# Seven-product weight slabs in two more MLPs of a three-block network, and a regrouping in the last MLP

## What is computed

```
first block, two layers:   x = x + mixer(x); x = x + relu(rms_norm(x, g) @ w_in)**2 @ w_out     # 4096 hidden
second block:              x = x + 0.5 * swiglu(rms_norm(x, g), w_gate, w_up, w_down)           # 2816 hidden, ffn1
                           x = x + mixer(x);  then the same swiglu again                        # ffn2
third block:               mod = silu(c) @ w_ada + b_ada       # 1024 x 6144, depends on c alone
                           x = layer_norm(alpha * x + (1 + g) * mixer(x))
                           x = layer_norm(alpha * x + (1 + g) * swiglu(h, w_ffn_in, w_ffn_out)) # ffn3
```

## Time and profile before

| | before |
|---|---|
| median of three runs | 3399.15 us |
| the profiled execution, device time | 3401.31 us |
| its span | 3399.5 us |
| PE busy | 3313.1 us (97%) |
| POOL busy | 1888.2 us (56%) |
| DVE busy | 1792.6 us (53%) |
| ACT busy | 880.2 us (26%) |
| granted TensorE clock, mean | 0.996 |
| DMA | 340.89 MB, mean 100 GB/s |

### The profile page before, as it was taken

How to read it: one execution, slowest core, us unless ns; L and a number is a source line. 1 busy time by engine, 2 the same in 40 slices (tenths; PEclk the granted TensorE clock), 3 DMA queues, 4 the chain that set the end, 5 groups by cost and what they waited for, 6 DMA issues and landing times.

```text
span 3399.5 us, 48354 instructions
## 1 busy us (share of the span) xinstructions
PE 3313.1 (97%) x20166; PEld 2664.7 (78%) x20166; DVE 1792.6 (53%) x2828; ACT 880.2 (26%) x1845; POOL 1888.2 (56%) x1499
## 2 busy tenths in 40 slices
PE   8999999999999999999999998999999999999997
PEld 6767788986778888888788777778887776778996
DVE  6544334548544344333442666564346657568775
ACT  2242011347411112000202532110002125235443
POOL 7526666731256666767675002777665645846652
PEclk9999999999999999999999999999999999999998
DMA  5203334230033432433323002432324635412321
GB/s 175 83 25 112 111 125 136 79 104 26 26 109 102 136 128 90 141 113 99 99 87 113 12 3 70 130 106 87 99 87 150 216 92 177 149 56 94 101 98 63
DMA packets 258970, 340.89 MB, mean 100 GB/s; under 512 B 9920, under 2 KB 196544, under 8 KB 256192
## 3 DMA queue, kind: packets, MB, share of 16 engines
q1 hardware_dynamic: 236240, 301.51, 27.3%
q10 hardware_dynamic: 22512, 36.28, 3.0%
HBM read 308.15 MB, written 25.43 MB: 98 GB/s over the span
## 4 chain that ended last, share of the span: by engine, by line
PE 87%; DVE 6%; POOL 3%; ACT 2%; DMA 1%; issue 1%; ACTq 0%; DVEq 0%; SPq 0%; POOLq 0%
PE bank L130 86%; PE bank L133 2%; POOL wlo L153 1%; DVE scr L153 1%; POOL whi L160 1%; DVE st L168 0%; POOL raw L153 0%; DMA sq<-gates 0%; DVE p L160 0%; ACT L148 0%; DMA raw<-in_w_mlp_in 0%; ACT ah L148 0%; DVE BK L153 0%; DVE al L163 0%; DVE x L153 0%
## 5 line engine op out<-in xcount | busy, mean ns | idle before, releaser
L153 POOL TENSOR_TENSOR wlo<-raw,whi 128x512 fp32r<-128x512 f32 x890 | 1221.4, 1403 | 121.6 <-ACT whi L148 103.8
L160 POOL TENSOR_SCALAR whi<-raw 128x1024 fp32r<-128x1024 f32 x425 | 484.2, 1157 | 1263.5 <-PE bank L130 577.4
L130 PE MATMUL bank<-ah,whi 128*128 128x512 f32 (+1 forms) x2408 | 925.0, 384 | 11.5 <-ACT ah L148 4.5
L130 PE MATMUL bank<-ah,wlo 128*128 128x512 f32 (+1 forms) x2408 | 917.7, 381 | 0.0
L130 PE MATMUL bank<-al,whi 128*128 128x512 f32 (+1 forms) x2408 | 906.5, 381 | 0.9 <-DVE al L163 0.9
L130 PEld LDWEIGHTS bank<-ah,whi 128*128 128x128 f32 x2408 | 451.7, 188 | 120.6 <-ACT ah L148 8.2
L130 PEld LDWEIGHTS bank<-al,whi 128*128 128x128 f32 x2408 | 451.4, 188 | 99.5 <-DVE al L163 1.8
L130 PEld LDWEIGHTS bank<-ah,wlo 128*128 128x128 f32 x2408 | 451.6, 188 | 96.9 <-issue 0.2
L130 PE MATMUL bank<-hh,whi 128*128 128x512 f32 x1040 | 412.4, 397 | 0.0
L130 PE MATMUL bank<-hl,whi 128*128 128x512 f32 x1040 | 410.8, 395 | 0.0
L130 PE MATMUL bank<-hh,wlo 128*128 128x512 f32 x1040 | 410.7, 395 | 0.0
(11 more groups left out here) (481 smaller groups left out, 4722.8 us busy)
## 6 DMA issues: line engine op xcount, KB each, us to landing
raw<-in_w_in SPq DMA_DIRECT2D x34, 1024.0 KB, 5.3
raw<-in_w_mlp_in SPq DMA_DIRECT2D x32, 1024.0 KB, 5.9
raw<-in_w_mlp_out SPq DMA_DIRECT2D x32, 1024.0 KB, 7.4
raw<-in_w_ada SPq DMA_DIRECT2D x24, 1024.0 KB, 5.3
raw<-in_ffn_w_gate SPq DMA_DIRECT2D x22, 1024.0 KB, 5.4
raw<-in_ffn_w_up SPq DMA_DIRECT2D x22, 1024.0 KB, 5.3
raw<-in_ffn_w_down SPq DMA_DIRECT2D x22, 1024.0 KB, 5.1
raw<-in_w_ffn_in SPq DMA_DIRECT2D x22, 1024.0 KB, 6.1
```

The source lines that it names most:

```text
L130: return self.eng.matmul(out, lhsT, rhs, start=start, stop=stop, skip_group_check=True)
L153: return IDLE if self.eng is None else self.eng.tensor_tensor(out, a, b, op)
L160: return self.eng.tensor_scalar(out, a, s1, s2, op0, op1)
```

## The change

The seven-product form is switched on by a table, for mlp1, ffn1 and ffn3, and its code serves ReLU and gated MLPs. Group 0 stays as it was in each.

```diff
+        squares = lambda prev: lambda: [self.D.at(prev, "xsq", 7)]
+        self.pairing = dict(
+            mlp1=Pairing(squares("out1"), p("norm_mlp_g1")), ffn1=Pairing(squares("mlp1"), p("ffn1_norm")),
+            ffn3=Pairing(lambda: [self.P.at("nffn3", "xsq", 7)], None))
...
+        def slabs(g):
+            steps = [(kind, p0, W) for p0 in range(0, len(groups[g]), 2) for kind, W in (("gate", gate), ("value", up)) if W]
+            m = 8 // len(steps)
+            for j, (kind, p0, W) in enumerate(steps):
...
+                self.pair_pe(e, (name, kind, g, p0), W[0], W[1] + 128 * groups[g][p0], way.ready, j == 0 and g == 1)
...
+                self.outs_pe(e, name, g - 1, down, len(groups[g - 1]), m * j, m, T)
+                if ada and (j + 1) % (len(steps) // 2) == 0:
+                    self.ada_pe(e)
```

A step has m down tiles in one transfer (`outs_pe`, `outs_high_act`, `outs_low_pool` take m): 4 in mlp1 (1 MB), 2 in ffn1 and ffn3 (0.5 MB), and 4 in the last group of the gated ones, where there were two transfers of 2. ACT's order, with `opens` true in an MLP's first paired step:

```diff
+            some(parts, opens)
+            self.outs_high_act(a, o)
             some(high, 1)
-            some(parts, 1)
-            some(high, 2)
+            some(parts, not opens)
+            some(high, 1 if opens else 2)
+            if before:
+                for i in range(before[1], before[1] + 2):
+                    hidden(a, name, T, before[0], i)
```

So P1 of the first slab is copied before the down weights' high copies, P5 before S1's high copy, and the hidden copies of group 0's last two tiles move behind them. DVE gets for `rooted` MLPs the multiplications with `rb` on the assembled tiles (`made`, two per step in ffn1, a ReLU with `rb` in mlp1), and the modulation's part at the end of a step:

```diff
+            elif gated:
+                d.wait_ge(*C.at(name, "silu", g, i))
+                d.wait_ge(*D.now())
+                t = d.tt(m[:, :], T["gt"][i][:, :], m[:, :], MUL)
+                if rooted:
...
+                    t = d.tt(m[:, :], m[:, :], self.rb[:, :], MUL)
+                t.then_inc(*D.up(name, "made", g, i))
+            else:
+                d.wait_ge(*D.now())
+                d.stt(m[:, :], m[:, :], 0.0, self.rb[:, :], MAX, MUL).then_inc(*D.up(name, "relu", g, i))
...
+            if ada and m * (j + 1) % 4 == 0:
+                self.ada_dve(d)
```

For mlp1 and ffn1 ACT makes the token blocks' source itself (eight copies of `x` times the gain, `pairs_begin_act`) and DVE their sums at the head of group 0; the rest of the opening is that of ffn3 (`pairs_high_act`, `pairs_low_dve`, `pairs_open_act`, `pairs_open_dve`), with the modulation's part of group 0 behind it:

```diff
+                    if way and p0 == (0 if way.gain else 2):
+                        self.token_sums_dve(d, name)
+                    if way and p0:
+                        low = self.pairs_low_dve(d, name)
...
+                if way:
+                    self.pairs_open_dve(d, name, low)
                 if ada:
                     self.ada_dve(d)
```

More of the change, by code:

```diff
@@ L1782, in mlp_pe @@
         for g in range(len(groups) + 1):
+            if paired(g):
+                slabs(g)
+                continue
             if g < len(groups):
                 first(g)
-                if g == len(groups) - 1 and not pairs:
+                if g == len(groups) - 1:
                     self.P.mark("used", name)
@@ new lines, in paired_dve @@
+        for j, kind, p0, s, o, before, opens, ends, m in self.pair_steps(name, gated, g, groups):
+            key = (name, kind, g, p0)
+            low = iter(()) if ends else self.pair_low_dve(d, s + 1)
+            if j:
+                adds(g - 1, m * (j - 1), m)
+            elif not opens:
+                adds(g - 2, 8 - (2 if gated else 4), 2 if gated else 4)
+            m1, m2 = [self.scr.take(name, "h", g, i)[0] for i in (p0, p0 + 1)] if gated and kind == "value" else \
+                [T["gt"][i] for i in (p0, p0 + 1)]
+            some(low, 3)
+            if before:
+                for i in range(before[1], before[1] + 2):
+                    hidden(d, name, T, before[0], i)
+            some(low, 2 if kind == "gate" or not gated else 1)
+            self.pair_first_dve(d, key, m1)
+            if kind == "gate":
+                made(kind, p0, p0, m1)
@@ L1931, in paired_dve @@
             some(low, 1)
-            self.pair_second_dve(d, (name, "gate", g, p0), m2)
-            D.mark(name, "gate", g, p0 + 1)
+            if kind == "value":
+                made(kind, p0, p0, m1)
+            self.pair_second_dve(d, key, m2)
+            made(kind, p0, p0 + 1, m2)
             run(low)
-            s += 1
-            last = not more and p0 + 2 == len(tiles)
-            low = iter(()) if last else self.pair_low_dve(d, s)
-            up = [self.scr.take(name, "h", g, i)[0] for i in (p0, p0 + 1)]
@@ L1950, in paired_dve @@
[L1950 to L1959 removed]
+            if ada and m * (j + 1) % 4 == 0:
+                self.ada_dve(d)
+        if ends:
+            for i in (p0, p0 + 1):
+                adds(g - 1, 8 - m + i - p0, 1)
+                hidden(d, name, T, g, i)
+            adds(g - 1, 8 - m + 2, m - 2)
@@ new lines, in pairs_begin_act, with pairs_high_act @@
+    def pairs_begin_act(self, a, name, gain):
+        a.wait_ge(*self.D.at(f"n{name}", 7))
+        for k in range(8):
+            a.f(self.tok_t["v"][k // 4][:, k % 4, :], self.x[:, k, :], ACT.Copy, scale=gain(k)).then_inc(
+                *self.C.up(name, "token value", k))
+    def pairs_high_act(self, a, name):
+        for n in (3, 4, 6):
+            self.tokens_high_act(a, name, n)
+        high = self.pair_high_act(a, self.pair_first.get(name, 0))
+        self.some(high, 4)
+        return high
```

321 lines of the change are left out of this document (139 added, 182 removed).

## The result

The changed kernel takes **3482.26 us** (median of four runs, 3478.97 to 3486.54) against 3399.61 us before in the same session (3399.05 to 3400.95). The ratio is 1.0243, with a 95% interval of 1.0226 to 1.0261: 2.4% slower, 82.7 us. The forecast had 3454 us and a range of 3412 to 3488. Sign and range held (the result lies near the upper end), the loss was half as large again as forecast. The profiled execution of the changed kernel is the slowest of its four, with a span of 3484.6 us.

The account below looks back on a forecast made before the run. PE's columns were taken to set the time (PE busy 97%). Terms -44.8 - 4 + 25 + 29 + 17 + 33 = +55 us on the profiled 3401.3 gave 3456.5, or 3454 us as median; range 3412 to 3488.

Parts of the forecast that it names:

- What is saved: mlp1 and ffn1: 32 slabs in seven-product form each take 9.8 us of PE instead of 11.2, -44.8 us.
- ffn3: ffn3: one transfer in place of two saves 6.1 us in the last group, the opening costs 2; net -4 us.
- mlp1's opening: mlp1's first paired slab: token work on DVE delays the third token block and slab 2, +29 us (24 to 33).
- mlp1's steps: mlp1's later steps: late modulation parts delay slabs, four times losses of 2.4, 2.1 and 1.8 us, +25 us.
- R: Any slab: the time its transfer lands after the start of the slab PE is working on.
- R - 2: Late slabs: approximate loss where the wait is not long enough for the clock to fall.
- ffn1's opening: ffn1's first paired slab: token work hidden in group 0, but slab 2 lands late and holds product 6, +17 us.
- ffn1's steps: ffn1's later steps: three modulation parts consumed after up steps each make a slab 11 us late, +33 us.
- R - 0.5: Late slabs: loss where the wait is long enough for the clock to fall.
- The columns decide: The three raw buffers: freed early enough, only token work of mlp1's opening is lost; 3361 us, chance 0.09.
- only the openings lose: mlp1 and ffn1: repeated late slabs are covered, the two openings are not; 3396 us, chance 0.06.
- Worse: Openings and late slabs: longer 1.2 GHz stretches and DVE delaying banks, about +90 us, 3489 us; chance 0.14.

Follow-up runs that it names:

- the last kernel: Changed kernel with the form from group 2, modulation parts at step heads and ahead of token work, additions and low parts before the last token block: 3377.93 us.

## Why the prediction was right, and where not

**What is saved: right.** Slabs on time take 9.80 us in mlp1 and ffn1. As the prediction asked, PE waits for ACT's copies from PSUM, 73.9 us from mlp1 to the end of ffn1.

**ffn3: right, -5.3 for -4.** The last group's late slab is gone (all slabs behind the first are 9.80 us, where one was 15.95). The opening costs 0.7 us more than before, not 2: PE waits once, for 5.2 us, where it waited three times.

**mlp1's opening: right, +29.8 for +29.** DVE's low part and the modulation part ended at 982.9 and 985.9 (982 and 986 forecast), the slab was there at 994.1 (993.3), the last product ended at 1002.7 (1002).

**mlp1's steps: the mechanism right, the size wrong, +40.4 for +25.** This is the step that failed. The rule for the loss, about R - 2, held: for the slabs right behind a modulation part R was 6.8, 5.4, 5.4 and 5.3 and the loss 5.3, 3.4, 3.9 and 3.2; for those two behind it R was 4.8 to 5.3 and the loss 2.7 to 3.3. But R was too small in the sum: 4.3 and 3.8 taken, 5.7 and 5.0 measured on average. For the first kind the part ended 0.15 us later than taken, SP issued the slab 0.44 us behind the end, behind the next part, and the slab landed 7.7 to 9.2 us after its issue. A single time to landing of 7.4 us from the earlier trace rows was taken for a constant; why one slab took 9.2 us is open. For the second kind the part ended 0.75 us later than taken: its four instructions took 4.9 us, where a mean of 1.05 from the earlier trace rows gave 4.2. The slab landed after 5.5 to 6.0 us instead of 5.3 (the transfer that the earlier trace rows calls alone had another one 0.4 us behind it). These late slabs lost 27.6 us instead of 18. The bank waits of 1.8 us were about right (1.5, four times), but five slabs behind late ones waited another 0.5 to 0.6 us for a bank, and one slab lost 1.7 us to the low clock. Together that is some 13 of the 15 us.

**ffn1's opening: the new slab right (15.4 us, R = 16.8), group 0 wrong.** "Group 0 has 44.8 us, so the token work is hidden": it is hidden in length, not in place. DVE's token sums stand ahead of the first gate tiles. DVE and PE after:

```profile
1374.26 4.54 DVE L153 TENSOR_TENSOR v<-v,v 128x1024 f32<-128x1024 f32 x2
1378.83 2.17 DVE L153 TENSOR_TENSOR v<-v 128x1024 f32<-128x1024 f32 x1
...
1381.66 0.79 PE L130 MATMUL bank<-ah,whi 128*128 128x512 f32 x1 [3.72 <-DVE gt L153]
```

PE waits 3.7 us for a bank that the multiplication behind the sums frees, and some 3 us more go at the low clock behind that wait (mean 0.88 from 1381.66 to the group's end at 1406.87): 7 us. The prediction did not ask what stands behind the sums on DVE.

**ffn1's steps: nearly right in the sum, +35.4 for +33, by two errors that cancel.** The three gate slabs lost 8.7, 7.9 and 9.2 us instead of 11, because DVE ended the part 3.8 to 4.0 us after the slab's start and not 6.1. R of 9.2, 9.1 and 9.5 gave these losses, R - 0.5 within 0.8 us. The 6.1 began with a slip: the next slab in the earlier trace rows starts at 3194.05, not 3194.25. Three up slabs that the prediction had charged nothing lost 4.0, 2.2 and 3.4, by the chain through the up slab's own buffer. That the sum came out is luck. The two errors may be linked, since PE's time lost in an up slab is time in which DVE catches up; no run separates them.

**The rivals.** "The columns decide" and "only the openings lose" fell. "Worse" gave 3489 us, nearer to the result than the forecast of 3454, and its mechanism is there in part. The low clock did not lengthen mlp1's opening beyond the forecast (29.8), but three of mlp1's later slabs ran in part at it (means 0.89, 0.88 and 0.85). Its other half, that DVE is never caught up and delays the banks, showed as the 0.6 us waits of mlp1, and in ffn1 once the transfers were taken away.

## What to carry to other kernels

Where a few buffers are handed round in one fixed order of transfers, a consumer's place in its engine's queue is a scheduling decision for every transfer behind it: consume in the order of loading. Here four instructions moved from the end of a step to its head, and one addition moved behind the next step's, were together worth 66 us, with no work saved. Count the buffers too: a transfer put between two others takes one away from them, and moving its consumer did not give that back (ffn1's up slabs). Ask of a stalled copy what stands before it and why: "first" for P1 looked like a cure and cost 190 us, because what stood before it filled a gap. And a first use (an opening) wants its own cover: starting one group later gave up 8 us of gain in columns and, once the same chain was mended there and the additions stood earlier, came out 38 us ahead (3416.25 to 3377.93).

## What the runs showed of the hardware that I had not expected

- The time to landing of 1 MB issued 0.4 us behind another one ranged from 7.7 to 9.2 us in one MLP of one run, where a third transfer followed within 2 us.
- The length of a wait alone does not tell whether the granted clock falls. Behind the same bank wait of 1.54 us in mlp1 the slab took 9.9 us at 1.00 or 11.3 to 11.5 us at 0.85: one of four was slow in the profile after, three of four when the same kernel ran again. A wait of 2.08 us left a slab at 1.00 (1136.48 to 1149.67), one of 2.05 us at 0.88 (1209.04 to 1222.71).
- Four multiply-adds of a modulation part took from 3.1 us in ffn1 up to 6.2 us on DVE while POOL worked (987.21 to 993.44 in the last kernel): one instruction's mean over a stage is no bound.
- Two executions of one program differed by 7.3 us in a single mixer, and DVE's waits for small transfers differed with them (15.5 and 6.8 us).
